# Two blocks of normalised, rotated queries turned by a DMA exchange of 32x32 squares in place of TensorE transposes

## The chip, the cores and the metric

One core of a Trainium2 chip runs the whole program. The metric is the device time in microseconds (us) of one execution; the runs of the kernel before stand in the table below. The inputs are float32 and lie in HBM, and so does the output.

## What is computed

Two transformer blocks, one after the other, on 256 tokens of width 1024. The first has two layers (retention and stick-breaking attention side by side, then a gated feed-forward layer). The second has two layers too, each with a half-weighted feed-forward, a mixer, a cross attention to 256 memory rows and another feed-forward. The change touches the mixer of the second block's layer 0, the even mixer:

```python
def even_mixer(h, w_in, f_bias, qk_gains, lam_params, subln_gain, lambda_init, w_out, cos, sin):
    a_q, a_k, a_v, a_f, b_q, b_k, b_v = split_cols(h @ w_in, EVEN_SIZES)
    aq = rms_norm(a_q.reshape(bsz, seq, A_HEADS, HEAD_DIM), qk_gains[0])
    ...
    a_out = forgetting_attention(aq, ak, av, cum_logf).reshape(bsz, seq, A_WIDTH)
    bq = rms_norm(b_q.reshape(bsz, seq, B_HEADS, 2, HEAD_DIM), qk_gains[2])
    bk = rms_norm(b_k.reshape(bsz, seq, B_HEADS, 2, HEAD_DIM), qk_gains[3])
    bq, bk = apply_partial_rope(bq, cos, sin), apply_partial_rope(bk, cos, sin)
    b_out = differential_attention(bq, bk, bv, lam)
    ...
    return jnp.concatenate([a_out, b_out], axis=-1) @ w_out
```

Both attentions need queries and keys with the feature on the partition axis, while the projections come out with the token on it. So each of bq, bk, aq and ak (256 tokens x 512 features) has to be turned. The forgetting attention adds a cumulative sum of log gates to its scores; its differential neighbour does not.

## The kernel before, in words

**Projections.** Every weight comes from HBM in units of 128x1024 floats (512 KB) into one of four RAW slots. ScalarE (ACT) rounds it to the high part WH (line 1311), VectorE (DVE) subtracts to get the low part WL (line 1593), and both lie in one of five slots. A 512-wide projection is a chunk of 4 units: TensorE (PE) takes three matmuls for each k tile and each of the two row tiles t (lines 1037 to 1039), 48 in all, into a pair of the four PSUM banks M. A RAW slot is filled again when its WL is made, a WH/WL slot when PE has used it.

**Order of the work.** The class Plan gives every step a time `at`, in units of one k tile of a 512-wide chunk (six matmuls, 1.30 us in the trace). PE and GpSimd (POOL) work through the steps in the order of `at`. ACT and DVE take `at` plus an offset for the kind of step, from the table LATER. The numbers in PLACES are offsets from the end of a chunk, and so set where a step stands in all these queues. Every engine works strictly in its order, and waits on semaphores.

**Queries and keys (head_qk).** ACT evicts the chunk into two TMP buffers (line 1354) and squares them (1358); DVE sums the squares (1804); ACT and DVE make the reciprocal root (1364 to 1367, 1742 to 1748); the step `hn` on DVE multiplies by it and, for bq and bk, applies gain and rotation in lines 1763 to 1788. Then there are two ways to turn the result:

- `turn_q` (step `tq`), used by bq, bk, aq and ak: four PE transposes for each row tile into an AUX bank (line 1095), and an eviction by ACT into QB, KB, QA or KA (line 1385).
- `heads_out` (steps `bt`, `sq_out`, `sq_in`, `tx`), used by dq, dk and others: DVE transposes 32x32 squares within a 128x512 tile (line 1711), twice; POOL issues one 512 KB DMA to HBM (2033), waits for its landing, and issues four 128 KB DMAs back (2046), which put the squares where they belong; ACT copies the result twice, once for each row tile (1415). One buffer holds the squares that go out, another those that come back.

**The stage.** Counting from the end of bq's chunk (0): the narrow chunk af, the gates, takes 2 units, bk runs from 2 to 10, bv from 10 to 18, aq from 18 to 26, ak behind it. In these units the steps around the change stand as follows. On PE: bq's two `tq` at 9.8, the sums of the gates `cu2` (lines 1185 to 1189) at 10, bk's two `tq` at 19.2 and 20.4, the first scores `df_s` of the differential attention (1199 to 1202) at 22.1, its transposed probabilities `pt` (1209) at 28. On POOL: `nctld` at 10.5, which writes the gates' sums to HBM (2103), waits for that, and reads them back spread over all partitions into NB (2106, 2107). On DVE: `nctma` at 26, which adds the causal mask to NB (2003) just ahead of `df_p`, the probabilities (1886 to 1898). On ACT, with offsets: the unit of `at` 18 is rounded, bk's evictions stand at 19.9 and 21.1 with the unit of 20 between them, then the unit of 22.

A TMP buffer is given to the first step that needs one once its last reader's place is past. Where that reader is a `bt`, the next writer waits for it (the function `vacant`).

Of the kernel before, what the change touches and what calls it, by code (L numbers as in the profile page):

```python
# [24 lines left out]
NTMP = 9  # L25
PARKED = 4
PLACES = {
# [5 lines left out]
    "df_p": (4.3, 4.6, 4.6, 4.6), "df_pt": (5.9, 6.8, 6.2, 6.8), "df_o": (7.4, 8.4, 9.9, 7.4),  # L33
    "bo": (28, 28.5, 29.2, 30.1, 34.4, 36.4), "hg_s": (1.3, 6.6, 11.6, 16.3), "hg_late": (1.3, 1.3, 1.3, 2.5),
    "hg_p": (3, 5.4, 4.2, 5.4, 4.2, 5.4, 4.2, 6.6), "hg_pt": (5.6, 6.8, 5.6, 6.2, 6.2, 7.4, 6.2, 7.7), "hg_o": (8.2, 7.6, 8.5, 8.5),
    "od_s": (0.3, 6, 9.8, 14.3), "od_late": (0, 1.3, -1.2, 1.3), "od_p": (3, 5.4, 4.2, 4.2, 1.7, 5.4, 4.2, 5.4),
# [213 lines left out]
class Plan:  # L250
# [132 lines left out]
    def turn_q(self, at, source, maker, x, key, form, dst, gain):  # L383
        s = self.add("xt" if form == "parts" else "tq", at)
        s.source, s.maker, s.x, s.form, s.dst, s.gain = source, maker, x, form, dst, gain
        s.half = 0
        x.final = s
        self.turned[key] = s
        return s
# [153 lines left out]
    def head_qk(self, c, norm, groups, lab, finish, room=None):  # L543

        s = self.evict_x("hq", c, norm)
        n = T * groups
        s.groups = groups
        s.ss, s.v = self.small(n), self.small(n)
        r_at, n_at, x_at, y_at = (c.end + x for x in PLACES[lab])
        r = self.rsqrt(r_at, s.v, n, s)  # L550
        f = self.add("hn", n_at)
        f.q, f.rs, f.groups, f.xs, f.first_use = s, r, groups, s.xs, True
        form, dst, gain, f.rope = finish
        if room is not None:
            assert f.rope is None
            self.heads_out(x_at, y_at, "hn", f, s.xs, *room, lab, form, dst, gain)
            return s
        for t, at in enumerate((x_at, y_at)):
            self.turn_q(at, "hn", f, s.xs[t], f"{lab}{t}", form, dst(t), gain).half = t
        return s  # L560
# [173 lines left out]
    def even_mixer(self, S, lab, lab_o):  # L734
        A, QA, KA, VA, QB, KB, VB, BO = (S[x] for x in ("A", "QA", "KA", "VA", "QB", "KB", "VB", "BO"))
        B, nm = self.B, self.norms[lab]
        cols = lambda dst: (lambda t: dst[:, :, t * P:(t + 1) * P])
        c = self.chunk("bq", B, 0, KD, lab)
        self.head_qk(c, nm, 8, "bq", ("plain", cols(QB), 0.125, 0))
        c = self.narrow("af", B, KD, lab)  # L740
        f = self.evict("af", c, nm)
        f.x = self.tmp(c.mms[-1])
        c1 = self.add("cu1", c.end + PLACES["cu"][0])
        c1.f, c1.x, c1.norm = f, f.x, nm
        f.x.final = c1
        c1.y, c1.ab, c1.lf = self.small(16), self.small(16), self.small(16)
        cl = self.add("cu_l", c.end + PLACES["cu"][1])
        cl.c1 = c1
        ct = self.add("cu2", c.end + PLACES["cu"][2])
        ct.l, ct.lf, ct.CT, ct.NCT = cl, c1.lf, S["CT"], S["NCT"]  # L750
        ld = self.add("nctld", c.end + PLACES["cu"][3])
        ld.ct, ld.rows, ld.NB = ct, S["NCT"], S["NB"]
        ma = self.add("nctma", c.end + PLACES["cu"][4])
        ma.NB = S["NB"]
        c = self.chunk("bk", B, 0, KD, lab)
        self.head_qk(c, nm, 8, "bk", ("plain", cols(KB), 1.0, 1))
        c = self.chunk("bv", B, 0, KD, lab)
        bv = self.values(c, nm, [VB[:, t, :] for t in range(T)])
        BS = self.small(8)
        e0 = c.end  # L760
        for h in range(4):
            b = e0 + PLACES["df_s"][h]
            ss = []
            for j in range(2):
                s = self.add("df_s", b)
                s.late = PLACES["df_late"][h] * j
                s.mate = ss[0] if j else None
                s.q, s.k = (x[64 * j:64 * j + 64, h, :] for x in (QB, KB))
                s.turned = [self.turned[x] for x in ("bq0", "bq1", "bk0", "bk1")]
                s.vals = bv  # L770
                s.m, s.sm, s.rc = self.small(2), self.small(2), self.small(2)
                s.e = self.tmp(s)
                ss.append(s)
            f = self.add("df_p", b + PLACES["df_p"][h])
            f.ss, f.nl = ss, self.small(2)
            t = self.add("pt", b + PLACES["df_pt"][h])
            ss[1].e.final = t
            t.source, t.maker, t.e = "df_p", f, ss[0].e
            ss[0].e.final = t
            t.x = self.tmp(t)  # L780
            o = self.add("df_o", b + PLACES["df_o"][h])
            o.pt = t
            t.x.final = o
            o.v = VB[:, :, h * P:(h + 1) * P]
            o.dst = [BO[:, t_, h * P:(h + 1) * P] for t_ in range(T)]
            o.bs = [BS[:, 4 * t_ + h:4 * t_ + h + 1] for t_ in range(T)]
        at = [e0 + x for x in PLACES["bo"]]
        v = self.add("bo_v", at[0])
        v.o, v.bs, v.v = o, BS, self.small(8)
        r = self.rsqrt(at[1], v.v, 8, v)  # L790
        for t in range(T):
            f = self.add("bo_n", at[2 + t])
            f.rs, f.first_use, f.x, f.t = r, t == 0, BO[:, t, :], t
        for j in range(2):
            blocks = [BO[:, t, (2 * j + q) * P:(2 * j + q + 1) * P] for q in range(2) for t in range(T)]
            self.turn(at[4 + j], "bo_n", f, blocks, A, 2 * j, None, lab_o, 2 * j)
        c = self.chunk("aq", B, 0, KD, lab)
        self.head_qk(c, nm, 8, "aq", ("plain", cols(QA), self.gq["a"], None))
        c = self.chunk("ak", B, 0, KD, lab)
        self.head_qk(c, nm, 8, "ak", ("plain", cols(KA), self.gk["a"], None))  # L800
        c = self.chunk("av", B, 0, KD, lab)
        av = self.values(c, nm, [VA[:, t, :] for t in range(T)])
        self.CT, self.ct = S["CT"], ct
        self.heads(c.end, "hg", lab_o, ["aq0", "aq1", "ak0", "ak1"], VA, QA, KA, av, S["NB"], A)
# [479 lines left out]
def scalar(e, k):  # L1284
    p = k.p
# [8 lines left out]
    for s in p.for_act:  # L1294
# [3 lines left out]
        if s.kind in ("rope", "vals", "valx", "plainx", "ff", "hq", "rg"):  # L1298
            c = s.c
# [29 lines left out]
        elif s.kind == "gate":  # L1329
            c = s.c  # L1330
# [19 lines left out]
        elif s.kind == "hq":  # L1350
            for t in range(T):
                vacant(e, k, s.xs[t])
                x = p.TMP[s.xs[t].i]
# [27 lines left out]
        elif s.kind == "tq":  # L1381
            e.wait_ge(k.aux_full[b], s.use)
            v = aux[:, :].rearrange("p (j c) -> p j c", j=4)
            if s.form == "plain":
                e.activation(s.dst, v, ACT.Copy, scale=s.gain).then_inc(k.aux_out[b], 1)
            elif s.form == "heads":
                e.wait_ge(k.zeroed, s.zero.n)
                e.activation(s.dst[0:64, 0:8:2], v[0:64], ACT.Copy, scale=s.gain[0:64])
                e.activation(s.dst[64:128, 1:8:2], v[64:128], ACT.Copy, scale=s.gain[64:128]).then_inc(k.aux_out[b], 1)
            else:  # L1390
                v4 = v.rearrange("p (h j) c -> p h j c", j=2)
                d4 = s.dst.rearrange("p (h j) c -> p h j c", j=2)
                e.activation(d4[:, :, 0, :], v4[:, :, 0, :], ACT.Copy, scale=s.gain[0])
                e.activation(d4[:, :, 1, :], v4[:, :, 1, :], ACT.Copy, scale=s.gain[1]).then_inc(k.aux_out[b], 1)
        elif s.kind == "hx":
            x = s.x
# [9 lines left out]
        elif s.kind == "tx":  # L1406
            x = s.x
# [65 lines left out]
        elif s.kind == "st_s":  # L1473
# [3 lines left out]
            x = p.TMP[s.z.x.i][:, 0:384]  # L1477
# [31 lines left out]
        elif s.kind in ("df_s", "hg_s"):  # L1509
# [4 lines left out]
            x = p.TMP[s.e.i]  # L1514
# [3 lines left out]
        elif s.kind == "cx_s":  # L1518
# [4 lines left out]
            x = p.TMP[s.e.i]  # L1523
# [12 lines left out]
        elif s.kind == "df_o":  # L1536
            e.wait_ge(k.aux_full[b], s.use)
            for t in range(T):
                x = aux[:, t * P:(t + 1) * P]
# [614 lines left out]
def build_program(nc, a, out, scratch, squares, parked_nct):  # L2154
    with ExitStack() as ctx:
# [134 lines left out]
        @block.scalar  # L2290
        def _(e):
            scalar(e, k)
# [44 lines left out]
```

## Time and profile before

| what | value |
|---|---|
| median of 3 runs | 1872.3 us (1871.98 to 1875.15) |
| the profiled execution, its own time | 1872.1 us |
| its span, first to last instruction | 1870.2 us |
| PE busy | 1863.4 us of the span, granted clock 1.00 |
| DVE busy | 1321.9 us |
| ACT busy | 1122.1 us |
| POOL busy | 353.6 us |
| DMA | 436.43 MB, 233 GB/s on average |

The profile names instructions by the line of the kernel and by the tile written and read; "idle before, releaser" is how long the engine stood before an instruction and what ended that. Times in the timeline are microseconds from the start of the span.

### The profile page before, as it was taken

The page shows a single profiled execution, that of the slowest core. Times are in us where ns is not written, and L with a number is a line of the kernel's source. Part 1 is how long each engine was busy: PE and PEld are TensorE (multiplying, and loading weights), DVE is VectorE, ACT ScalarE, POOL GpSimd, SP SyncE. Part 2 cuts the span into 40 slices and gives each one's busy share as a digit, 9 for nine tenths or more (in the row PEclk, how much of TensorE's full clock was granted, in tenths as well). Part 3 has the DMA queues.
Part 4 walks back from the last instruction along what each step waited for, and adds up shares of the span by engine and source line. Part 5 has one row for each costly group of instructions (what it writes and reads, how often), then busy time and mean ns, then how long its engine had stood idle before and what let it go on. Part 6 is the DMA issues. An engine that isn't in the chain of part 4 may idle for free.

```text
span 1870.2 us, 25364 instructions
## 1 busy us (share of the span) xinstructions
PE 1863.4 (100%) x9283; PEld 1625.1 (87%) x9283; DVE 1321.9 (71%) x1941; ACT 1122.1 (60%) x1682; POOL 353.6 (19%) x590
## 2 busy tenths in 40 slices
PE   9999999999999999999999999999999999999999
PEld 8888988888889888888888789888888888899888
DVE  6776776667776776666578986776666578877664
ACT  6776655557766655555467785654555467765552
POOL 2100233111001441132100001531122011102320
PEclk9999999999999999999999999999999999999999
DMA  9867789877578997798765556997788787648884
GB/s 314 239 187 220 223 259 304 256 233 256 168 213 241 290 289 233 218 270 258 237 183 179 172 190 203 277 280 238 224 255 254 217 273 232 214 147 241 254 258 137
DMA packets 289659, 436.43 MB, mean 233 GB/s; under 512 B 25532, under 2 KB 170144, under 8 KB 289280
## 3 DMA queue, kind: packets, MB, share of 16 engines
q1 hardware_dynamic: 260240, 352.41, 61.7%
q0 software_dynamic: 28832, 82.07, 16.1%
q8 instruction: 74, 1.21, 0.3%
q14 instruction: 49, 0.40, 0.1%
q10 hardware_dynamic: 464, 0.34, 0.1%
HBM read 396.43 MB, written 38.29 MB: 232 GB/s over the span
## 4 chain that ended last, share of the span: by engine, by line
PE 97%; DVE 2%; ACT 0%; issue 0%; DVEq 0%; ACTq 0%
PE M L1037 31%; PE M L1039 30%; PE M L1038 30%; PE AUX L1081 1%; DVE WL L1593 1%; PE AUX L1095 0%; PE AUX L1209 0%; PE M L991 0%; ACT WH L1311 0%; PE AUX L1251 0%; PE AUX L1279 0%; PE AUX L1278 0%; PE AUX L1252 0%; PE AUX L1253 0%; PE AUX L1280 0%; PE AUX L1124 0%
## 5 line engine op out<-in xcount | busy, mean ns | idle before, releaser
L1593 DVE TENSOR_TENSOR WL<-RAW,WH 128x1024 fp32r<-128x1024 f32 (+1 forms) x670 | 811.3, 1216 | 382.2 <-ACT WH L1311 380.1
L1311 ACT ACTIVATE WH<-RAW 128x1024 fp32r<-128x1024 f32 (+1 forms) x670 | 706.1, 1056 | 526.1 <-PE M L1039 483.0
L1037 PE MATMUL M<-WH,Bh 128*128 128x512 f32 (+1 forms) x1822 | 692.0, 380 | 0.5 <-DVE WL L1593 0.5
L1038 PE MATMUL M<-WL,Bh 128*128 128x512 f32 (+1 forms) x1822 | 683.9, 375 | 0.0
L1039 PE MATMUL M<-WH,Bl 128*128 128x512 f32 (+1 forms) x1822 | 683.9, 375 | 0.0
L1037 PEld LDWEIGHTS M<-WH,Bh 128*128 128x128 f32 x1822 | 344.6, 189 | 49.1 <-issue 2.0
L1039 PEld LDWEIGHTS M<-WH,Bl 128*128 128x128 f32 x1822 | 344.5, 189 | 47.2
L1038 PEld LDWEIGHTS M<-WL,Bh 128*128 128x128 f32 x1822 | 344.7, 189 | 44.8
L1349 ACT ACTIVATE AS<-M,KEEP 128x256 f32<-128x256 f32 x132 | 55.4, 471 | 79.9 <-PE M L1039 78.4
L1037 PE MATMUL M<-WH,MTh 128*128 128x512 f32 x128 | 50.9, 398 | 0.0
L1038 PE MATMUL M<-WL,MTh 128*128 128x512 f32 x128 | 48.5, 379 | 0.0
L1039 PE MATMUL M<-WH,MTl 128*128 128x512 f32 x128 | 48.5, 379 | 0.0
L2033 POOL DMA_DIRECT2D squares<-QT x4 | 3.1, 763 | 175.6 <-DVE QT L1711 175.6
L2046 POOL DMA_DIRECT2D HB0t<-squares x48 | 26.4, 557 | 48.9 <-DMA squares<-HB0b 40.3
L2046 POOL DMA_DIRECT2D HB1t<-squares x48 | 26.5, 558 | 45.9 <-DMA squares<-HB1b 34.7
L2046 POOL DMA_DIRECT2D HC0t<-squares x48 | 26.4, 557 | 45.3 <-DMA squares<-HC0b 44.3
L1684 DVE SCALAR_TENSOR_TENSOR X<-M,X 128x512 f32<-128x512 f32 (+1 forms) x54 | 30.5, 607 | 6.0 <-PE M L1039 6.0
L2046 POOL DMA_DIRECT2D HD0t<-squares x48 | 26.5, 559 | 42.6 <-DMA squares<-HD0b 32.8
L2046 POOL DMA_DIRECT2D HC1t<-squares x48 | 26.4, 556 | 39.9 <-DMA squares<-HC1b 36.2
L1446 ACT ACTIVATE JK<-X 128x512 f32<-128x512 f32 x52 | 32.7, 629 | 1.4 <-DVE X L1684 0.5
L2026 POOL TENSOR_TENSOR KEEP<-SM,KEEP 128x2 f32<-128x2 f32 x15 | 12.6, 839 | 110.7 <-DVE SM L1669 101.2
L1037 PE MATMUL M<-WH,FA0h 128*128 128x512 f32 x88 | 33.4, 379 | 0.0
(530 smaller groups left out, 2885.4 us busy)
## 6 DMA issues: line engine op xcount, KB each, us to landing
RAW<-in_ffn_w_in SPq DMA_DIRECT2D x352, 256.0 KB, 4.1
RAW<-in_w_in SPq DMA_DIRECT2D x103, 512.0 KB, 4.7
RAW<-in_w_gate_up SPq DMA_DIRECT2D x176, 256.0 KB, 4.4
RAW<-in_ffn_w_out SPq DMA_DIRECT2D x88, 512.0 KB, 4.5
RAW<-in_w_down SPq DMA_DIRECT2D x44, 512.0 KB, 4.8
RAW<-in_x_w_kv SPq DMA_DIRECT2D x32, 512.0 KB, 4.3
RAW<-in_even_w_in SPq DMA_DIRECT2D x24, 512.0 KB, 4.5
RAW<-in_odd_w_in SPq DMA_DIRECT2D x24, 512.0 KB, 5.4
```

What stands on the lines that cost most here:

```text
L1037: e.matmul(out, s.hi, wh, start=s.at0, stop=False)
L1038: e.matmul(out, s.hi, wl, start=False, stop=False)
L1039: i = e.matmul(out, s.lo, wh, start=False, stop=s.final)
L1081: tr = e.transpose(aux[:, i * P:(i + 1) * P], x, ident)
L1311: e.activation(p.WH[:, h, 0:s.size], p.RAW[:, i, 0:s.size], ACT.Copy).then_inc(k.w_hi, 1)
L1349: e.activation(s.silu[t], banks[t][:, 0, :], ACT.Silu, scale=r[t]).then_inc(k.silu_made, 1)
L1446: e.activation(p.JK, s.srcs[t], ACT.Square, accum_out=s.ss[:, 2 * t + s.half:2 * t + s.half + 1]).then_inc(k.sq_sum, 1)
L1593: e.tensor_tensor(p.WL[:, h, 0:s.size], p.RAW[:, s.u % NRAW, 0:s.size], hi.bitcast(F32), ALU.subtract).then_inc(k.w_lo, 1)
L1684: e.scalar_tensor_tensor(out=x, in0=banks[t], scalar=s.scale, in1=x, op0=ALU.mult, op1=ALU.add).then_inc(k.m_out[c.banks[t]], 1)
L2026: e.tensor_tensor(s.r, s.v, p.MHALF, ALU.pow).then_inc(k.r_made, 1)
L2033: e.dma_start(p.parked[x.slot, 0:4 * P * 32 * x.m].rearrange("(c p e) -> p c e", c=n, p=P), x.squares.rearrange("p (c e) -> p c e", c=n)). ...
L2046: e.dma_start(x.rows[32 * c:32 * c + 32, :].rearrange("p (q e) -> p q e", q=q), p.parked[x.slot, c * n:(c + 1) * n].rearrange("(q j e) -> ...
```

## The change

bq is turned by `heads_out` instead of `turn_q`. The squares go out from QA's memory and come back into KA's; both are idle until aq and ak are turned. `bt` stands at 7 and `tx` at 18.6 after the end of bq's chunk. Three steps are moved a little: `cu2` from 8 to 8.3 after af's end (10 to 10.3 in the count above), the first `pt` from 5.9 to 6.1 and the first `df_o` from 7.4 to 7.6 after their `df_s`. The field `clear` is set to None everywhere and the wait on it is never emitted.

```diff
-    ... "bq": (3.2, 3.5, 9.8, 9.8),
+    ... "bq": (3.2, 3.5, 7, 18.6),
-    ... "cu": (1, 2, 8, 8.5, 24), ...
-    "df_p": (4.3, 4.6, 4.6, 4.6), "df_pt": (5.9, 6.8, 6.2, 6.8), "df_o": (7.4, 8.4, 9.9, 7.4),
+    ... "cu": (1, 2, 8.3, 8.5, 24), ...
+    "df_p": (4.3, 4.6, 4.6, 4.6), "df_pt": (6.1, 6.8, 6.2, 6.8), "df_o": (7.6, 8.4, 9.9, 7.4),
@@ turn_q
-        s.half = 0
+        s.half, s.clear = 0, None
@@ head_qk
         if room is not None:
-            assert f.rope is None
             self.heads_out(x_at, y_at, "hn", f, s.xs, *room, lab, form, dst, gain)
@@ even_mixer
+        rows = lambda x: [Rows(x.rearrange("p k c -> p (k c)"))]
         c = self.chunk("bq", B, 0, KD, lab)
-        self.head_qk(c, nm, 8, "bq", ("plain", cols(QB), 0.125, 0))
+        self.head_qk(c, nm, 8, "bq", ("plain", cols(QB), 0.125, 0), (rows(QA[:, :, :]), rows(KA[:, :, :])))
@@ scalar, step tq
+            if s.clear is not None:
+                e.wait_ge(k.tx_made, s.clear.n)
```

## Rows read from the trace of the kernel before

**Rows 1.** The page: busy time by engine, and the chain that ended last.
```profile
PE 1863.4 (100%) x9283; PEld 1625.1 (87%) x9283; DVE 1321.9 (71%) x1941; ACT 1122.1 (60%) x1682; POOL 353.6 (19%) x590
...
PE 97%; DVE 2%; ACT 0%; issue 0%; DVEq 0%; ACTq 0%
```

**Rows 2.** The waits of PE over the whole run: total us, times, longest.
```profile
PE AUX L1209 <- DVE TMP L1909: 1.3, 1, 1.3
...
PE AUX L1209 <- DVE TMP L1898: 0.3, 1, 0.3
```

**Rows 3.** The timeline of PE around the stage: start, us, engine, line, what.
```profile
966.82 1.04 PE L1095 MATMUL AUX<-CC,TMP 128*128 128x128 f32 x8
967.79 0.60 PE L1185 MATMUL AUX<-C,SM 128*8 128x256 f32 x2
...
981.61 0.60 PE L1095 MATMUL AUX<-CC,TMP 128*128 128x128 f32 x4
...
986.47 0.37 PE L1199 MATMUL AUX<-KB,QB 64*128 64x128 f32 x1
...
996.04 0.55 PE L1209 MATMUL AUX<-CC,TMP 128*128 128x128 f32 x3 [0.27 <-DVE TMP L1898]
```

**Rows 4.** The timeline of DVE in the stage.
```profile
966.87 3.49 DVE L1593 TENSOR_TENSOR WL<-RAW,WH 128x1024 fp32r<-128x1024 f32 x3
...
979.67 0.22 DVE L1788 TENSOR_TENSOR TMP<-VT 128x64 f32<-128x64 f32 x1
...
987.42 0.43 DVE L1863 TENSOR_TENSOR AUX<-AUX,C 128x256 f32<-128x256 f32 x1 [2.14 <-PE AUX L1201]
...
991.87 2.35 DVE L2003 TENSOR_TENSOR NB<-NB,C 128x1024 f32<-128x1024 f32 x2
```

**Rows 5.** The timeline of ACT in the stage.
```profile
968.05 0.67 ACT L1354 ACTIVATE TMP<-M,KEEP 128x512 f32<-128x512 f32 x1
...
970.53 1.07 ACT L1385 ACTIVATE QB<-AUX 128x512 f32<-128x512 f32 x2
...
981.03 1.06 ACT L1311 ACTIVATE WH<-RAW 128x1024 fp32r<-128x1024 f32 x1
982.25 0.60 ACT L1385 ACTIVATE KB<-AUX 128x512 f32<-128x512 f32 x1 [0.16 <-PE AUX L1095]
...
983.98 0.60 ACT L1385 ACTIVATE KB<-AUX 128x512 f32<-128x512 f32 x1
```

**Rows 6.** Timelines of DVE and ACT: start of a 512 KB exchange, and its first reader.
```profile
1300.99 1.30 DVE L1711 STREAM_TRANSPOSE HD0b<-X 128x512 f32<-128x512 f32 x2
...
1315.59 1.71 ACT L1404 ACTIVATE Bh<-HD0t,GTt 128x256 fp32r<-128x256 f32 x4 [0.27 <-DMA HD0t<-squares]
...
363.82 1.30 DVE L1711 STREAM_TRANSPOSE HB0b<-X 128x512 f32<-128x512 f32 x2
...
379.90 1.71 ACT L1404 ACTIVATE Bh<-HB0t,GTt 128x256 fp32r<-128x256 f32 x4 [1.76 <-DMA HB0t<-squares]
...
1532.56 1.30 DVE L1711 STREAM_TRANSPOSE SQO<-TMP 128x512 f32<-128x512 f32 x2
...
1550.74 1.34 ACT L1415 ACTIVATE KD<-SQI,GTt 128x512 f32<-128x512 f32 x2 [3.15 <-DMA SQI<-squares]
```

**Rows 7.** The timeline of POOL in dk's exchange.
```profile
1534.40 0.77 POOL L2033 DMA_DIRECT2D squares<-SQO  x1 [1.62 <-DVE SQO L1711]
1542.05 2.19 POOL L2046 DMA_DIRECT2D SQI<-squares  x4 [6.87 <-DMA squares<-SQO]
```

**Rows 8.** The timeline of ACT: the two copies of an exchange without a gain column.
```profile
43.22 1.14 ACT L1415 ACTIVATE SQ<-TG 128x512 f32<-128x512 f32 x2
```

**Rows 9.** POOL's timeline and the DMA issues (us to landing): the gates' rows.
```profile
972.20 0.55 POOL L2103 DMA_DIRECT2D forget_rows<-NCT  x1 [22.47 <-ACT CT L1508]
975.85 0.92 POOL L2106 DMA_DIRECT2D NB<-forget_rows  x1 [3.10 <-DMA forget_rows<-NCT]
...
NB<-forget_rows POOLq DMA_DIRECT2D x1, 1024.0 KB, 8.1
```

4 rows, old and new, of the table PLACES are left out of this document.

## The prediction, made before the changed kernel was built or run

> **What bounds the kernel now.** I read the page first. PE is busy in 1863.4 of 1870.2 us and the chain that ended last is 97% PE [rows 1]: every microsecond off or onto PE's queue is one of the kernel, and other engines count only where they make PE wait. So the next view is the list of PE's waits. In the stage of the change PE waits once, 0.3 us, for the first probabilities of the differential attention; the only other wait behind the start that is worth a step is one of 1.3 us some 600 us later [rows 2], in a part the change only shifts. Then I read the timelines of PE, DVE, ACT and POOL from 955 to 1000 us, to see what stands where the steps go.
>
> **PE: what is removed.** The two `tq` of bq are eight transposes from 966.82; `cu2` starts at 967.79 [rows 3]. So 0.97 us leave PE's queue, about 0.12 a transpose, since they overlap. TensorE: Matmul & The Clock Gate of the Trainium skill, Part 4 (PE-mode transpose), gives about 275 ns for one in a kernel's context; eight of these end to end would be 2.2 us, and by that estimate rival A below would end at 1869.6; the row disagrees. `cu2` at 10.3 stands behind one tile of bv: its operand, which DVE makes just ahead of 966.87 [rows 4], would come too close if PE arrived 0.97 us sooner, so no wait is added and none removed. The term is -0.97.
>
> **PE: the first `pt`.** It waits 0.27 us at 996.04 [rows 3]. What it waits for is one closed run of DVE that starts with the first scores (987.42) and ends with the probabilities [rows 4]; both ends hang on `df_s`, so the wait doesn't change when `df_s` moves. At 6.1 instead of 5.9 `pt` stands behind one more tile of ak, three matmuls or 0.65 us. The wait goes, with 0.38 us to spare. The term is -0.27. `df_o` is moved past one tile as well, costs nothing, and nobody waited for it.
>
> **DVE: two square transposes more.** 1.30 us for the pair [rows 6]. By the offsets `bt` (7.5 on DVE) stands behind the WL of the unit of 6 (6.9) and ahead of that of 8. At 966.87 DVE makes three WL in a row, 1.13 us apart, since the rotation had held it [rows 4]; the first of the three is that of 6. So `bt` runs from 968.0 to 969.3, and PE's saving doesn't move it, because DVE is behind here. The WL behind it come 1.3 us later; the next of them is made at 970.4 and is that of bv's last unit, which begins 6 units (7.8 us) after bv does, at about 976: over 5 us of cover. If that were gone, up to 1.3 us would come onto PE.
>
> **ACT: one wait early, harmless.** bq's TMP buffers are now free at 7, so bk takes the same ones, and its eviction, at 968.05 before [rows 5], waits for `bt`: it starts at about 969.4. The two QB evictions, 1.07 us at 970.53 [rows 5], are gone from there, which gives most of it back. Following the queue (evict, square, `cu2`, one WH, root) bk's rotation starts 0.3 us later and ends at 980.2 instead of 979.89 [rows 4]. PE's transposes of bk, at 981.61 before [rows 3], now come at 980.64. 0.4 us remain: cost 0; if my sum is 1 us short it is 0.6.
>
> **ACT: the wait that decides.** `tx` stands at 18.6, behind the WH that ran from 981.03 to 982.09 [rows 5]. What precedes that WH waited for PE, so it moves with PE: ACT is at `tx` at 982.09 - 0.97 = 981.1. Behind `tx`, on ACT, are both KB evictions with a WH between them, 982.25 to 984.58, that is 2.3 us [rows 5], and behind them `df_s` on PE. The squares must have landed. The trace has no exchange in this place, so I bound it by the six 512 KB exchanges whose landing ACT waited for, and so shows. From the start of the DVE transposes to the landing they took 14.6 us at the least, 16.1 in the middle and 18.2 at the most; those three stand in [rows 6] (the three between were 15.1, 16.9 and 16.9). They are biased upwards, because only a late one is waited for; I take 15.9. The ends are 14.0, a little under the shortest, and 18.2. Landing: 968.0 + 15.9 = 983.9. Then `tx`, 1.1 us [rows 8], and 2.3 us of KB: `df_s` can start at 987.3. PE would be there at 986.47 - 0.97 = 985.5. **PE waits 1.8 us** (0 to 4.1). While the wait lasts, ACT also holds the WH of the unit of 20, which PE needs in its next chunk, at 28, beside the first `pt` (996 before).
>
> DMA: Bandwidth & Descriptors of the Trainium skill (Anatomy of one DMA) fits 2.0 us plus bytes over 436 GB/s for a DMA of GpSimd. That is 3.2 us out and 2.3 us for each piece back, and with the issues in between it puts the landing some 9 us after `bt` starts, an estimate from that page. In [rows 7] the way out alone took 7.6 us.
>
> **POOL.** The exchange stands ahead of `nctld`. From the issue of the way out to the first issue back is 7.65 us in dk's case and the four issues back take 2.2 [rows 7]; from an issue at 969.8 POOL is held until 979.7. The gates' rows, which went at 972.20, go then. The read back starts 3.65 us later, its larger part is issued 0.9 us on and lands in 8.1 us [rows 9]: 992.3. `nctma` on DVE, at 991.87 [rows 4], moves by what `df_s` moves, 987.3 - 986.5 = 0.8, to 992.7, so it just doesn't wait. Cost 0; if NB lands 2 us later still, 1.6 us on DVE and, less the 0.38 in `pt`, 1.2 on PE. The exchange adds 0.5 MB out and 0.5 MB back among the weight loads; with four RAW and five WH slots ahead of PE I cost that at 0, and a late load would show as a wait of PE for WL.
>
> **The sum**, against the profiled execution's own 1872.1 us (span 1870.2 and 1.9 around it; the median of the runs shown is 0.2 above it): 1872.1 - 0.97 - 0.27 + 1.8 = 1872.7. Where the wait binds, the transposes' price cancels: the start of `df_s` is set by the landing, and what PE saves ahead of it, PE waits.
>
> **The rivals.**
> A, the exchange is in time. If the squares land by 982.1, 14.1 us after `bt` starts, `df_s` is not held: 1872.1 - 1.24 = 1870.9. For it: the six are biased, and the shortest misses by only 0.5 us. Against it: all six took longer. Chance 0.28.
> The page on DMA named above, of the Trainium skill, leads to the same time, by its 9 us.
> B, slower: the exchange is as late as dk's. 18.2 us [rows 6] put the landing at 986.2, PE's wait at 4.1 and the time at 1875.0. It would be over 0.2% slower from a landing 19 us after `bt` on. For it: the weight loads that waited for DVE behind the rotation go out just ahead of the squares. Chance 0.16, about half of it beyond 1875.8.
> C, the gates' rows bind: the squares are in time, but NB lands at 992.3 as worked out above, while DVE, not held at `df_s`, is at `nctma` at 991.87 - 0.97 = 990.9. It waits 1.4 us, PE 1.0 at `pt`: 1871.9. Chance 0.06.
> The forecast, a wait of 0.4 to 3.2 us, has 0.50.
>
> **How the numbers follow.** 0.2% is 3.7 us, about what a measurement of this kernel can tell from no change. All PE could give here is 1.24 us and perhaps the 1.3 us wait far behind, so faster by over 0.2% gets 0.02. Slower by over 0.2% needs nearly 5 us of wait: 0.08. Within: 0.90. The range goes from just under A, 1870.5, to just past B, 1875.4.
>
> **What would show it.** Right: L1095 has eight matmuls less; L1711 shows QA<-TMP at about 968.0, 1.30 us; ACT's L1415 QB<-KA has a wait for KA<-squares before it and starts near 983.9; PE waits before L1199 for ACT KB, 1 to 3 us, and not at all at the first L1209; bk's L1354 waits for QA. Wrong: L1415 without a wait (A), a wait of PE or DVE with NB as its releaser (C), or PE standing at L1037 for a WL in the stage, which would mean that DVE's cover is not there.

## The result, and the profile after

Slower: 1877.76 us median (9 runs, 1876.93 to 1880.18) against 1872.30 us for the kernel before on the same chip (9 runs). The ratio is 1.003, with a 95% interval of 1.0022 to 1.0039, so the loss is 5.5 us, give or take 1.6. The forecast of 1872.7 was wrong, and so was the range, whose upper end was 1875.4.

The profiled execution took 1880.18 us, the longest of the nine, with a span of 1878.4: 8.2 us more than before. Of these, 2.3 are already there at 955 us, ahead of anything the change touches, in waits of the earlier stages such as the 1.2 us at L1115 below. The change touches nothing there, and the median execution is 2.4 us shorter than this one, so I take them as a matter of this one execution: times of this trace have to be read less 2.3 us to be set beside those of before. The other 5.9 come behind 955.

The page after, to be set beside [rows 1]:

```profile
PE 1865.2 (99%) x9275; PEld 1625.8 (87%) x9275; DVE 1323.2 (70%) x1943; ACT 1120.6 (60%) x1682; POOL 356.8 (19%) x595
...
PE 92%; DVE 3%; DMA 2%; ACT 1%; issue 1%; POOL 0%; ACTq 0%; DVEq 0%; POOLq 0%
```

PE has its eight instructions less (9275 for 9283). But the chain is no longer almost all PE: DVE, DMA and ACT are in it with 6%. The waits of PE over the whole run say where (before: [rows 2]):

```profile
PE AUX L1209 <- DVE TMP L1900: 4.3, 1, 4.3
PE AUX L1209 <- DVE TMP L1911: 1.3, 1, 1.3
PE AUX L1115 <- ACT KT L1417: 1.2, 1, 1.2
```

The first row is the wait for the first probabilities, 0.3 us before and 4.3 now. Its cause is on DVE (before: [rows 4]):

```profile
970.28 1.30 DVE L1713 STREAM_TRANSPOSE QA<-TMP 128x512 f32<-128x512 f32 x2
...
992.20 1.23 DVE L1595 TENSOR_TENSOR WL<-RAW,WH 128x1024 fp32r<-128x1024 f32 x1
997.99 2.36 DVE L2005 TENSOR_TENSOR NB<-NB,C 128x1024 f32<-128x1024 f32 x2 [4.57 <-DMA NB<-forget_rows]
```

DVE stood 4.57 us with the gates' mask (`nctma`, now L2005), because NB had not landed, and the probabilities are queued behind it. Why NB was late shows on POOL (before: [rows 9]):

```profile
972.13 0.79 POOL L2035 DMA_DIRECT2D squares<-QA  x1 [20.12 <-DVE QA L1713]
978.50 2.19 POOL L2048 DMA_DIRECT2D KA<-squares  x4 [5.58 <-DMA squares<-QA]
980.68 0.53 POOL L2105 DMA_DIRECT2D forget_rows<-NCT  x1
984.94 0.92 POOL L2108 DMA_DIRECT2D NB<-forget_rows  x1 [3.72 <-DMA forget_rows<-NCT]
986.61 0.89 POOL L2109 DMA_DIRECT2D NB<-forget_rows  x1 [0.74 <-issue]
```

The exchange stands ahead of the gates' rows, and POOL idles in it for 5.58 us. NB's larger part goes at 986.61, at 984.3 in the time of before, where it had gone at 976.8. Then it takes 11.4 us instead of 8.1 (DMA issues of 970 to 1005: what, queue, KB, median us to landing):

```profile
RAW<-in_even_w_in SPq DMA_DIRECT2D x10, 512.0 KB, 6.4
NB<-forget_rows POOLq DMA_DIRECT2D x1, 1024.0 KB, 11.4
```

The squares themselves were in time. ACT (before: [rows 5]) waits 0.94 us for them, and no wait of PE at `df_s` is listed:

```profile
971.67 0.69 ACT L1354 ACTIVATE TMP<-M,KEEP 128x512 f32<-128x512 f32 x1 [1.18 <-DVE QA L1713]
...
984.50 1.15 ACT L1417 ACTIVATE QB<-KA 128x512 f32<-128x512 f32 x2 [0.94 <-DMA KA<-squares]
```

What follows the wait is seen in stretches of 2 us (busy time of PE, PEld, DVE, ACT, POOL; the granted clock; DMA share; GB/s):

```profile
998.00:1000.00 2.00, 0.00 (x0) 0.00 (x0) 2.00 (x2) 1.71 (x3) 0.00 (x0) 1.00 0.45 166
1000.00:1002.00 2.00, 0.00 (x0) 0.00 (x0) 1.90 (x8) 0.00 (x0) 0.00 (x0) 0.75 0.02 7
1002.00:1004.00 2.00, 1.84 (x6) 1.66 (x7) 1.97 (x5) 0.86 (x5) 0.00 (x0) 0.50 0.00 0
1004.00:1006.00 2.00, 2.00 (x6) 1.55 (x6) 1.97 (x6) 1.17 (x6) 0.00 (x0) 0.50 0.29 75
1006.00:1008.00 2.00, 2.00 (x10) 1.82 (x9) 1.93 (x6) 1.19 (x3) 0.00 (x0) 0.54 0.53 187
1008.00:1010.00 2.00, 2.00 (x12) 1.48 (x10) 1.97 (x6) 1.34 (x9) 0.00 (x0) 1.00 0.49 145
```

```profile
1002.16 0.90 PE L1209 MATMUL AUX<-CC,TMP 128*128 128x128 f32 x3 [4.27 <-DVE TMP L1900]
```

While PE stands, its granted clock falls to half, 1.2 GHz, and stays there until nearly 1008, although PE is busy again from 1002.16. At half speed it loses half of the 3.84 us that it is busy up to 1006, and 0.46 of the 2.0 us behind: 1.92 and 0.92, in all 2.84 us. So the time is accounted for: -0.97 for the transposes, -0.27 for the old wait, +4.27 for the new one, +2.84 for the clock, in sum +5.87 of the 5.9. All nine executions had a mean clock of 0.998 or 0.999, so this wasn't a peculiarity of the profiled one.

### The profile page after: what moved, and what is told of

Its sections match the earlier page's. It is cut to its first block, busy times and chain, and to the rows that moved or that the text cites. A ratio compares the mean times of both kernels' runs of the same rounds, so it can differ in the third digit from the quotient of the medians.

```text
span 1878.4 us, 25354 instructions
## 1 busy us (share of the span) xinstructions
PE 1865.2 (99%) x9275; PEld 1625.8 (87%) x9275; DVE 1323.2 (70%) x1943; ACT 1120.6 (60%) x1682; POOL 356.8 (19%) x595
## 4 chain that ended last, share of the span: by engine, by line
PE 92%; DVE 3%; DMA 2%; ACT 1%; issue 1%; POOL 0%; ACTq 0%; DVEq 0%; POOLq 0%
PE M L1037 29%; PE M L1039 29%; PE M L1038 29%; DVE WL L1595 1%; PE AUX L1081 1%; DMA NB<-forget_rows 1%; DMA RAW<-in_w_in 0%; DMA RV<-squares 0%; DMA squares<-QA 0%; ACT WH L1311 0%; DMA squares<-RV 0%; PE AUX L1095 0%; PE AUX L1209 0%; PE AUX L1251 0%; DMA forget_rows<-NCT 0%
## 5 line engine op out<-in xcount | busy, mean ns | idle before, releaser
L2048 POOL DMA_DIRECT2D HB1t<-squares x48 | 26.5, 558 | 50.2 <-DMA squares<-HB1b 41.6
L2048 POOL DMA_DIRECT2D HD0t<-squares x48 | 26.5, 559 | 45.3 <-DMA squares<-HD0b 45.3
```

What stands on the lines that cost most here:

```text
L2048: e.dma_start(x.rows[32 * c:32 * c + 32, :].rearrange("p (q e) -> p q e", q=q), p.parked[x.slot, c * n:(c + 1) * n].rearrange("(q j e) -> ...
```

## The experiments

The theory: the loss is NB, which the exchange on POOL's queue makes late, and the clock behind the wait. What the trace leaves open is why the transfer took 3.3 us longer, whether the exchange would be worth anything without it, and what the clock costs. All were timed in five rounds beside the kernel before, whose median was 1872.5 to 1872.9 us in them. This table goes ahead of the details, with NB's larger part, ACT's waits for RAW between 970 and 1000, and PE's idle time from 955 to 1030, all from the profiled executions. These are single ones and can lie off the median (after 1880.18 us, mask_late 1874.58, rows_late 1876.18, rows_gated 1870.56). The 986.6 of after is to be read less 2.3. PE's 0.7 in before_mask_late and its 0.9 in write_first_mask stand at 1013, the second 0.3 of rows_first at 1025, all three before a later `pt` and not before the first.

| run | NB issued | its transfer | ACT for RAW | PE idle | median us | ratio, 95% |
|---|---|---|---|---|---|---|
| before | 976.8 | 8.1 | 1.6 | 0.3 | 1872.3 | |
| after | 986.6 | 11.4 | 3.2 | 4.3 | 1877.76 | 1.0022 to 1.0039 |
| mask_late | 984.0 | 12.3 | 7.2 | 2.3 | 1872.74 | 0.9994 to 1.0012 |
| before_mask_late | 977.0 | 8.5 | 2.4 | 0.7 | 1872.91 | 0.9992 to 1.0009 |
| rows_first | 980.0 | 9.8 | 1.7 | 10.3 + 0.3 | 1882.07 | 1.0040 to 1.0065 |
| pe_wait_long | 977.7 | 8.3 | 2.0 | 4.2 | 1878.31 | 1.0019 to 1.0042 |
| pe_wait_short | 977.2 | 8.1 | 1.8 | 0.6 | 1873.12 | 0.9996 to 1.0014 |
| rows_late | 983.6 | 12.2 | 5.2 | 3.9 | 1877.94 | 1.0016 to 1.0040 |
| rows_late_mask | 984.2 | 11.8 | 4.8 | 1.5 | 1874.27 | 1.0000 to 1.0018 |
| rows_gated | 1001.8 | 10.7 | 2.1 | 0 | 1871.96 | 0.9985 to 1.0003 |
| before_rows_gated | 1004.9 | 10.2 | 0 | 0 | 1871.99 | 0.9988 to 1.0006 |
| write_first | 979.4 | 7.2 | 5.0 | 1.9 | 1874.48 | 0.9996 to 1.0014 |
| write_first_mask | 979.7 | 7.7 | 5.0 | 0.9 + 0.5 | 1873.79 | 0.9997 to 1.0015 |

### Does DVE's wait for NB make the loss? The mask later, after and before

```
 (the kernel after: run mask_late; before, run before_mask_late, has 8 for 8.3)
-"cu": (1, 2, 8.3, 8.5, 24)
+"cu": (1, 2, 8.3, 8.5, 26.5)
```

> The changed kernel with the mask on NB (line 2005 there) placed at 28.5 instead of 26, behind the first probabilities. Theory 1 (NB lands late, DVE stands at the mask, PE idles 4.3 us and the clock halves behind it): NB landed at about 995.7 in the time of the kernel before, DVE gets to the mask at about 997, so no wait; PE's wait at the first L1209 is gone, the clock stays at 1.00, and the time is 1870.9 us, 7 below the changed kernel and 1.2 to 1.4 below the kernel before. Theory 2 (the exchange itself costs: its traffic, DVE's 1.3 us, ACT's waits): PE still waits at L1209 or elsewhere in the stage, 1875 us or more.

> The kernel before with the mask moved in the same way: the control. Theory 1: only the 0.27 us wait at the first L1209 goes, 1872.0 us, so that the exchange is worth the 0.97 us of the eight transposes between this run and the one with both. Theory 2: the move of the mask is a gain by itself of 1 us or more, and the exchange is worth nothing or less.

With the mask behind the first probabilities the loss is gone within what can be told: 1872.74. Moving it in the kernel before gains nothing (1872.91). The move isn't free there: the 0.27 us wait is gone, but one of 0.73 us stands before a later `pt`, at 1013. So the 5.5 us hang on DVE's wait. But it isn't the 1870.9 that the first theory asked for. In mask_late PE stands at `df_o`, and ACT waits for weights:

```profile
PE AUX L1220 <- issue: 2.3, 1, 2.3
```

```profile
ACT WH L1311 <- DMA RAW<-in_even_w_in: 7.2, 3, 3.5
...
999.36 0.48 ACT L1534 ACTIVATE TMP<-AUX 128x384 f32<-128x384 f32 x1
```

The profile names no releaser for this wait, but in the kernel `df_o` needs ACT's eviction of the transposed probabilities (L1534). It ends at 999.84, PE starts at 999.94, and ACT has had no idle time since its last late weight, at 994.19.

The clock is in this execution too. Three of the eleven had a mean clock of 0.999 and took 1874.58 to 1876.26 us, the profiled one among them; the eight with 1.0 took 1872.01 to 1872.82. Behind the wait, from 997.68 to 999.94, the rows show half speed for 3.4 us in sum, so 1.7 us lost:

```profile
1000.00:1002.00 2.00, 2.00 (x11) 1.83 (x12) 1.97 (x3) 2.00 (x9) 0.00 (x0) 0.84 0.01 5
1002.00:1004.00 2.00, 2.00 (x5) 1.09 (x4) 1.93 (x9) 0.76 (x6) 0.00 (x0) 0.50 0.12 43
1004.00:1006.00 2.00, 2.00 (x13) 1.58 (x13) 1.84 (x5) 0.00 (x0) 0.00 (x0) 0.81 0.60 219
```

What PE waited for in the eight others no trace shows.

Neither theory had this: the weight loads are late too, for which I had allowed nothing.

### POOL's order the other way round

```
-        self.add("sq_in", at + 2.6).x = x
+        self.add("sq_in", at + (3.8 if source == "hn" and maker.rope is not None else 2.6)).x = x
```

> The changed kernel with POOL's order changed alone: the four DMAs that bring the squares back are put behind the three of the gates' rows. Theory 1: NB lands some 6 us earlier, the mask doesn't wait, and the squares come about 1.5 us later, which makes ACT wait and PE 0 to 1.5 us at L1199: 1870.9 to 1872.4 us, clock 1.00. Theory 2: no change against the changed kernel, 1877.8 us.

Both theories failed. NB, issued at 980.0, is no longer waited for. The squares' way back, issued right behind NB's 1.5 MB on the same queue, has a median of 7.7 us to landing instead of 3.8, and the last piece is far later: ACT waits 11.6 us for it and PE 10.3 for ACT.

```profile
ACT QB L1417 <- DMA KA<-squares: 11.6, 1, 11.6
```

In both orders the transfer that stands second on POOL's one queue comes too late: NB in the changed kernel, the squares here.

### What is a wait of PE worth?

```
 (the kernel before; 361 in pe_wait_long, 360 in pe_wait_short)
         elif s.kind in ("nctma", "hmask"):
+            if s.kind == "nctma":
+                e.wait_ge(k.w_used, 361)
```

> The kernel before, with no exchange and NB early, where the mask waits until PE has done the last matmul ahead of the first L1209. PE then idles for the mask and the probabilities, 4.3 us, as in the changed kernel. Theory 1, with the clock: the granted clock falls to 0.5 for about 7 us behind the wait and costs 2.8 us more: 1872.1 - 0.3 + 4.3 + 2.8 = 1878.9 us. Rival (the loss of clock in the changed kernel comes from something else in it): 1876.1 us, clock 1.00.

> The kernel before with nctma on DVE held by a semaphore until PE has used the weights one tile of ak earlier than in the 4.2 us case: PE should wait about 1.7 us at the first L1209 instead of 4.2. Theory 1 (a short idle leaves the clock at 2.4 GHz and costs its own length): +1.4 us, 1873.6 to 1874. Theory 2 (any idle of over 1 us brings the lower clock level): +1.4 and 1.7 to 3.4 more, 1875 to 1877.

A wait of 4.2 us on this spot, with every transfer as before, costs 5.9 us (1878.31 against 1872.46): 3.9 more of idle time, and 1.7 for the clock, which is at half speed for 3.4 us in sum by the windows of this run:

```profile
1000.00:1002.00 2.00, 1.23 (x6) 1.12 (x7) 1.97 (x6) 0.65 (x2) 0.00 (x0) 0.87 0.00 0
1002.00:1004.00 2.00, 2.00 (x6) 1.55 (x6) 1.97 (x5) 0.78 (x5) 0.00 (x0) 0.50 0.02 7
1004.00:1006.00 2.00, 2.00 (x12) 1.77 (x11) 1.97 (x4) 0.79 (x4) 0.00 (x0) 0.78 0.74 255
```

The short case missed its aim: PE waited 0.6 us instead of 1.7, so it doesn't tell the two theories apart. It says only that 0.6 us leave the mean clock of all eleven runs at 1.0, and the time where it was.

### The late issue alone, without the exchange

```
 (the kernel before; rows_late_mask also has "cu": (1, 2, 8, 8.5, 26.5))
         elif s.kind == "nctld":
+            e.wait_ge(k.w_used, 356)
```

> The kernel before, without any exchange; POOL issues the gates' rows (NB) only once PE has used the weights up to aq's first unit, about 979.6, so the 1024 KB go at about 984.2 instead of 975.9: as late as the exchange made POOL. This takes the late issue apart from the exchange's own traffic. Theory 1 (the transfer took 11.4 us instead of 8.1 because the exchange's pieces share its queue and the engines): here it takes 8 to 9 us and lands at 992 to 993, nctma on DVE waits under 1.5 us, PE under 1, the time is 1872.1 to 1873.5. Theory 2 (it took 11.4 us because of what else, weight loads, runs at that time): landing at about 995.6, DVE waits some 3.7 us, PE 3.4, the clock falls, the time is 1876 to 1878.

> The kernel before, without an exchange, with NB issued 8.5 us later (as in the run rows_late) and the mask at 26.5 units instead of 24 (as in mask_late). In mask_late, which has the exchange and the same NB, ACT waited 7.2 us for weights (RAW) and PE 2.3 us at 1000. Theory 1 (the rows' 1.5 MB issued late crowd the weight loads by themselves): ACT waits about 5 us for RAW here too, as in rows_late, PE waits 1 to 2.3 us ahead of 1000, the time is 1873.4 to 1875. Theory 2 (the exchange's extra 1 MB is what makes the weights late enough to matter): ACT's waits for RAW don't reach PE, 1872.1 to 1873.

This is the run that decides. There is no exchange in it, and the transposes are all there. Only POOL goes to the gates' rows as late as after.

```profile
980.75 0.55 POOL L2104 DMA_DIRECT2D forget_rows<-NCT  x1 [30.75 <-PE M L1039]
982.69 0.92 POOL L2107 DMA_DIRECT2D NB<-forget_rows  x1 [1.39 <-DMA forget_rows<-NCT]
983.60 0.89 POOL L2108 DMA_DIRECT2D NB<-forget_rows  x1
```

```profile
RAW<-in_even_w_in SPq DMA_DIRECT2D x8, 512.0 KB, 7.4
NB<-forget_rows POOLq DMA_DIRECT2D x1, 1024.0 KB, 12.2
```

The transfer takes 12.2 us, PE stands 3.9, and the median is 1877.94: theory 2, and all of the change's loss. So the 3.3 us extra do not come from the exchange's own megabyte. They come from the moment of the issue. The time of NB's larger part as one window, in the kernel before and then in rows_late, shows with how much else it ran:

```profile
976.76:984.86 8.10, 8.10 (x43) 7.10 (x42) 7.25 (x17) 5.51 (x7) 0.90 (x2) 1.00 0.93 308
983.60:995.80 12.20, 12.20 (x67) 9.65 (x65) 5.70 (x11) 5.58 (x13) 0.89 (x2) 1.00 1.03 338
```

At 308 GB/s the engines moved 2.5 MB in the 8.1 us, at 338 GB/s 4.1 MB in the 12.2. NB's two reads are 1.6 MB of either; the rest, 0.9 and 2.5 MB, is nearly all weights. The windows of the kernel before show what is there: the DMA engines have room just when NB used to start, and are full in the stretch that it starts in now (columns as above, the last but one is the DMA share):

```profile
974.00:976.00 2.00, 2.00 (x11) 1.73 (x10) 1.86 (x6) 1.06 (x1) 0.15 (x1) 1.00 0.45 92
976.00:978.00 2.00, 2.00 (x11) 1.76 (x10) 1.93 (x8) 0.66 (x1) 1.66 (x2) 1.00 0.83 268
...
984.00:986.00 2.00, 2.00 (x11) 1.75 (x10) 1.23 (x1) 0.58 (x2) 0.00 (x0) 1.00 1.05 370
986.00:988.00 2.00, 2.00 (x14) 1.28 (x13) 0.54 (x2) 1.06 (x1) 0.00 (x0) 1.00 1.06 390
```

My reading of these rows, which no run tests by itself: DVE converts no weights while it rotates bk, the RAW slots stay full and the loads pause; behind the rotation they catch up, and NB, which had the trough, now runs among them. The trace of before bears it out. Between 970 and 990 the queue of the weight loads waits for DVE's WL, once for 6.2 us:

```profile
SPq L2130 <- DVE WL L1593: 17.7, 7, 6.2
```

What the run shows is the 12.2 us, and a median of 7.4 us for the weight loads of 970 to 1005 instead of 5.1.

rows_late_mask has a PE wait of 1.5 us at `df_o` and 4.8 us of ACT's waits for RAW, where mask_late had 2.3 and 7.2. So late rows alone, without an exchange, make late weights and a wait at `df_o`: theory 1, and the 1874.27 lies inside the 1873.4 to 1875 expected. How much of mask_late's 2.3 and 7.2 is the exchange's stays open: these are two single executions, and the medians go the other way (mask_late 1872.74, with the exchange).

### The rows out of the way

```
 (the kernel after; before_rows_gated: the same two edits in the kernel before)
-"cu": (1, 2, 8.3, 8.5, 24)
+"cu": (1, 2, 8.3, 8.5, 39.5)
         elif s.kind == "nctld":
+            e.wait_ge(k.w_used, 362)
```

> The kernel with the change; the gates' rows are issued later still (POOL waits for the weights of ak's first chunk but one, about 987.5) and everything on DVE and ACT that needs them (the mask's part of cu) is moved from 24 to 39.5 units, behind the differential attention's first part. So no wait for NB can stand ahead of the first probabilities, and its 1.5 MB don't run beside the weight loads of 980 to 992. Theory 1 (the change itself is worth its transposes, and the loss is NB's alone): 1870.9 to 1872, no wait at the first L1209, and RAW waits on ACT back to about 1.6 us in sum. Theory 2 (the exchange's traffic by itself makes weight loads late): PE still waits 1 to 3 us at 1000 for ACT, 1872.5 to 1875.

> The control of the run above: the kernel before with the same later issue of the gates' rows and the same place of the mask. If moving them costs and gains nothing by itself: 1872.0 to 1872.6. If the rows collide with something behind 990 (the moved mask in front of the second half's probabilities), over 1873.5.

The exchange stays and NB leaves the stretch: PE has no wait left in the stage, ACT waits 2.1 us for RAW and harms nobody. `df_s` starts at 985.37, and at 986.75 in the control:

```profile
985.37 0.37 PE L1199 MATMUL AUX<-KB,QB 64*128 64x128 f32 x1
```

```profile
986.75 0.37 PE L1199 MATMUL AUX<-KB,QB 64*128 64x128 f32 x1
```

By 0.5 of these 1.4 us that execution was ahead already at 942 us, before the stage:

```profile
942.05 1.29 DVE L1686 SCALAR_TENSOR_TENSOR X<-M,X 128x512 f32<-128x512 f32 x2 [0.21 <-PE M L1039]
```

```profile
942.54 1.29 DVE L1684 SCALAR_TENSOR_TENSOR X<-M,X 128x512 f32<-128x512 f32 x2 [0.21 <-PE M L1039]
```

The other 0.9 are the change's, close to the 0.97 of the transposes. So up to `df_s` the exchange of squares gives about what it was sized at. The timing can't confirm it: 1871.96 and 1871.99, each within some 1.7 us. The interval of rows_gated against the kernel before reaches from 0.9985 to 1.0003: the best version found, not shown to be faster than the kernel before.

### The write early, the reads behind the squares

```
+        st = self.add("nctst", qe + PLACES["bq"][2] + 2.5)
+        st.ct, st.rows = ct, S["NCT"]
         ld = self.add("nctld", c.end + PLACES["cu"][3])
...
+        elif s.kind == "nctst":
             e.wait_ge(k.aux_out[s.ct.bank], s.ct.use)
             e.dma_start(p.parked_nct, s.rows[0:8, :]).then_inc(k.d_nct, 16)
+        elif s.kind == "nctld":
             e.wait_ge(k.d_nct, 16)
```

(`qe` is the end of bq's chunk; write_first_mask also has the mask at 26.5.)

> The kernel with the change, and one more edit on POOL: the 8 KB write of the gates' rows (forget_rows) goes between the exchange's way out and its way back, as POOL idles there for the landing; NB's two reads stay behind the way back. So NB no longer waits for that write's own round trip and is issued at about 980.7 and 981.6 instead of 984.9 and 986.6, into the stretch of 982 to 985 in which the engines of the DMA had room. Theory (the loss is the moment of NB's issue alone; behind the way back of the squares it does not matter that they share a queue): it lands before 991 to 992, in 8 to 10 us, DVE waits for it less than 1 us, PE less than 0.5 at the first L1209, the squares are as early as before (ACT at 984.5), the time is 1870.9 to 1872.0. Rival (with the exchange's traffic and 1.5 MB of rows in one stretch the late transfer is merely someone else's): NB lands after 994 all the same or ACT waits 3 us or more for weights at 989; 1873 to 1877.

> The run above with the mask's place at 26.5 units instead of 24 as well, behind the DVE work for the first probabilities. If the theory holds this adds nothing: 1870.9 to 1872.0, no wait of PE at the first L1209. If what is left in the run above is NB landing a little late, this is faster than it by that wait, up to 1 us. If ACT's waits for weights are what is left, both are alike at 1873 or more.

NB goes at 979.4, lands in 7.2 us and DVE doesn't wait for it, as the theory had it. The DMA engines are full here too, but little else runs beside the rows: 305 GB/s for 7.2 us are 2.2 MB, 1.6 of them NB's.

```profile
979.37:986.57 7.20, 7.20 (x42) 5.86 (x41) 5.14 (x7) 4.57 (x7) 0.89 (x1) 1.00 1.00 305
```

Yet PE waits 1.9 us and the median is 1874.48, a little beyond the 1872.0 it gave and inside the rival's. ACT's timeline shows the reason:

```profile
981.62 1.15 ACT L1420 ACTIVATE QB<-KA 128x512 f32<-128x512 f32 x2 [0.75 <-DMA KA<-squares]
...
987.68 1.06 ACT L1314 ACTIVATE WH<-RAW 128x1024 fp32r<-128x1024 f32 x1 [3.00 <-DMA RAW<-in_even_w_in]
990.74 1.06 ACT L1314 ACTIVATE WH<-RAW 128x1024 fp32r<-128x1024 f32 x1 [2.00 <-DMA RAW<-in_even_w_in]
```

The squares' way back and the rows' 1.5 MB now run one right behind the other, and the weights come late: two WH are 5.0 us late in sum, the WL and the mask behind them on DVE begin at 991.83 and 992.97, the latter 1.1 us later than in the kernel before although NB is there. The kernel before, which has no exchange and issues NB 2.6 us earlier, has 1.6 us of RAW waits. Which of the two differences makes the 5.0 isn't shown: no run has NB at this moment without an exchange. The clock is at half for 3.4 us in this execution too, from 997.5, behind an idle time of 1.94 us:

```profile
998.00:1000.00 2.00, 2.00 (x6) 1.64 (x5) 1.97 (x5) 1.30 (x5) 0.00 (x0) 0.50 0.00 0
```

With the mask moved, PE waits 0.5 us at `df_o` and 0.9 at 1013, and the median is 1873.79; the two intervals overlap, and the two runs can't be told apart.

## Why the prediction was wrong

**The transposes, -0.97: right.** Eight matmuls less, and `df_s` 0.9 us earlier in rows_gated against its control, offset taken out. **The first `pt`, -0.27: right as a step** (0 in rows_gated), void in the changed kernel, where a larger wait took its place.

**DVE: right.** `bt` at 970.28 is 968.0 in the time of before, for 1.30 us, and no PE wait for a WL came of it. **ACT's early wait: right.** bk's eviction waits 1.18 us for QA and starts at 971.67 (969.4).

**ACT: the wait that decides, +1.8: wrong, and it decided nothing.** ACT came to `tx` at 981.3 (predicted 981.1), but the squares had landed 14.2 us after `bt` began, not 15.9: rival A's case. What failed here is the choice of 15.9, close to the middle of six exchanges which, as the text itself said, are biased upwards, since only late ones are waited for. The 9 us worked out from DMA: Bandwidth & Descriptors of the Trainium skill (Anatomy of one DMA) pointed to the right case, but the durations disagree: the way out took 6.1 us here, not 3.2.

**POOL: the step that failed.** "Its larger part is issued 0.9 us on and lands in 8.1 us [rows 9]: 992.3 ... Cost 0." The moment of the issue was right to 0.1 us (984.3 against 984.2), and that was luck: POOL came to the rows at 978.4 and not 979.7, but the first read went 4.3 us after that and not 3.65, and the second 1.7 behind the first and not 0.9. The duration wasn't right: 11.4 us. I took it from a transfer that had run in a trough of the DMA, and moved it by 7.6 us into a full stretch without changing it; rows_late shows that the moment alone makes it 12.2. Rival C was the right mechanism with this one number wrong. With 11.4 its own sum gives 4.7 us for DVE and, less the 0.38, 4.3 for PE; measured were 4.57 and 4.27. With 8.1 it gave 1.0 and 1871.9, and a chance of 0.06.

**The exchange's bytes "at 0": open, and not what made this result.** In rows_gated, with no rows beside it, 0 holds: PE has no wait. Beside the rows, PE waits 1.9 us in write_first, where the kernel before has 0.3, but that one also issues NB 2.6 us earlier. What the prediction did miss is a price for late rows on the weight loads: in rows_late and rows_late_mask, with no exchange, ACT waits 5.2 and 4.8 us for RAW instead of 1.6.

**The clock: left out.** Every wait was priced at its own length. After 4.27 us of idle time PE ran at half clock for so long that 2.84 us more were lost; pe_wait_long has 1.7 for 4.2. Without this term C's corrected sum is 1872.1 - 1.24 + 4.3 = 1875.2, inside my range; with it 1878.0, against 1877.76 measured. So the number missed the range by this term, and the mechanism was missed by the 3.3 us of NB. Nothing in the trace of before had an idle time of that length in it, so it could not be priced, but its possibility should have pushed the slower end out.

Of the signs named for being wrong, one came: "a wait of PE or DVE with NB as its releaser (C)". Of those for being right, only the ones that tell of the steps came (eight matmuls less, `bt` at 968.0, bk's eviction waiting for QA). PE had no wait before L1199, `tx` started at 982.2 and not near 983.9, and the wait came at the first L1209, where none was to be.

## What to carry to other kernels

Before you put a step ahead of another on a queue, ask what the DMA engines are doing at the moment to which the second is pushed: a duration from the trace belongs to its place, and a transfer that fitted a trough took half as much again in the stretch behind it. Give a transfer that is moved its price in that stretch, also for what shares the engines with it, and look for the in-order engine whose queue stands behind its reader. And where PE is the bound, a wait of 2 to 4 us can cost 1.7 to 2.8 us more than its length.

## What was not expected of the hardware

The length of the idle time alone does not tell what the clock does. In write_first and mask_late it fell to half behind 1.94 and 2.26 us, for 3.4 us. In rows_late PE stood 3.9 us in the profiled execution, and its clock stayed at the full 2.4 GHz behind it; that execution took 1876.18 us and another with a mean clock of 1.0 took 1875.55. The four with a mean of 0.998 or 0.999 took 1877.13 to 1879.97. So the spread of that kernel, 4.4 us where the kernel before spreads over 2.3 in the same rounds, is probably in good part the clock's; how long PE stood in the five executions without a trace is not known.

```profile
998.00:1000.00 2.00, 0.04 (x1) 0.04 (x1) 1.90 (x9) 1.71 (x3) 0.00 (x0) 1.00 0.04 13
1000.00:1002.00 2.00, 2.00 (x11) 1.81 (x12) 1.97 (x5) 1.31 (x5) 0.00 (x0) 1.00 0.00 0
1002.00:1004.00 2.00, 2.00 (x14) 1.84 (x13) 1.97 (x6) 0.93 (x5) 0.00 (x0) 1.00 0.37 101
```

And the pieces of the squares' way back, 128 KB each, came with a median of 3.8 us alone and 7.7 behind 1.5 MB on the same queue (rows_first), and ACT waited 11.6 us for the last.

What stays open is why the clock fell after 1.94 us in one execution and not after 3.9 in another. Of the eleven executions of rows_late_mask, whose profiled one stood 1.5 us at the full clock, two had a mean of 0.999 and were the two slowest (1875.85 and 1877.5 us), so it may fall after less than 1.94; with 0.6 us, in pe_wait_short, none of eleven shows it.
